# Three weight chunks per layer loaded once and split on chip, and a shorter warm-up, in a two-layer hybrid encoder

## What is computed

```python
def hybrid_layer(x, ...):                     # x: 512 tokens x 1024, float32
    z = rms_norm(x, g) @ w_in                 # 1024 -> 3712
    aq, ak, av, ag, bq, bk, bv, bg, ca, cb, cg = split(z)
    ya = neighbourhood_attention(aq, ak, av, rpb) * silu(ag)         # 4 heads
    yb = dilated_attention(rotary(bq), rotary(bk), bv) * silu(bg)    # 6 heads
    yc = conformer_conv(ca, cb, w_dw, ..., w_pw, b_pw) * silu(cg)    # 384 channels, 31 taps
    return x + concat([ya, yb, yc]) @ w_out   # 1024 -> 1024

def reference(x, ...):
    for l in range(2):
        x = hybrid_layer(x, ...)
    return rms_norm(x, final_g)
```

## Time and profile before

| | us |
|---|---|
| median of 3 runs | 513.06 (511.6 to 513.33) |
| profiled execution, its own time | 513.21 |
| its span | 511.4 |
| TensorE busy | 501.6 (98%) |
| VectorE busy | 365.1 (71%) |
| ScalarE busy | 275.5 (54%) |
| POOL busy | 164.0 (32%) |
| q0 (POOL's transfers) | 62.93 MB, 54.3% of the 16 DMA engines |
| q1 (SP's transfers) | 34.02 MB, 23.1% |

### The profile page before, as it was taken

One profiled execution on the slowest core, in us unless ns is written; L12 is line 12 of the kernel. 1 busy time (PEld: TensorE's weight loads), 2 busy tenths in 40 slices (PEclk: granted clock), 3 DMA queues, 4 the chain that ended last, 5 costly groups with the idle time before them and its releaser, 6 DMA issues.

```text
span 511.4 us, 10279 instructions
## 1 busy us (share of the span) xinstructions
PE 501.6 (98%) x3998; PEld 401.9 (79%) x3998; DVE 365.1 (71%) x741; ACT 275.5 (54%) x531; POOL 164.0 (32%) x224
## 2 busy tenths in 40 slices
PE   8999999999999999999999999999999999999995
PEld 6888877887777778788888887878787877778883
DVE  6999978899984666521539878887999656852424
ACT  6844667664664475524425447676646646752314
POOL 0013332221143557425411333222122355663101
PEclk9999999999999999999999999999999999999998
DMA  8715889669986997999502378975999979899964
GB/s 292 308 43 132 198 210 207 132 162 204 232 215 159 236 251 168 245 237 278 159 2 82 88 163 196 214 174 102 220 219 223 226 166 266 217 243 247 203 169 164
DMA packets 55120, 97.79 MB, mean 191 GB/s; under 512 B 19872, under 2 KB 33696, under 8 KB 55072
## 3 DMA queue, kind: packets, MB, share of 16 engines
q0 software_dynamic: 19648, 62.93, 54.3%
q1 hardware_dynamic: 35136, 34.02, 23.1%
q10 hardware_dynamic: 288, 0.19, 0.1%
HBM read 84.92 MB, written 5.90 MB: 178 GB/s over the span
## 4 chain that ended last, share of the span: by engine, by line
PE 93%; DMA 4%; issue 1%; ACT 0%; DVE 0%; POOL 0%; POOLq 0%; SPq 0%; ACTq 0%; DVEq 0%
PE acc L607 22%; PE acc L608 21%; PE acc L609 21%; PE sc L718 5%; PE tp L751 4%; DMA w_lo<-w_out 3%; PE misc L782 2%; PE sc L669 2%; PE sc L607 1%; PE sc L609 1%; PE sc L608 1%; PE sc L670 1%; PE sc L671 1%; PE misc L777 1%; PE acc L647 1%
## 5 line engine op out<-in xcount | busy, mean ns | idle before, releaser
L607 PE MATMUL acc<-act_hi,w_hi 128*128 128x512 f32 x480 | 194.5, 405 | 0.1
L608 PE MATMUL acc<-act_hi,w_lo 128*128 128x512 f32 x480 | 187.7, 391 | 0.0
L609 PE MATMUL acc<-act_lo,w_hi 128*128 128x512 f32 x480 | 187.1, 390 | 0.0
L607 PEld LDWEIGHTS acc<-act_hi,w_hi 128*128 128x128 f32 x480 | 90.2, 188 | 21.9 <-issue 3.9
L609 PEld LDWEIGHTS acc<-act_lo,w_hi 128*128 128x128 f32 x480 | 90.2, 188 | 19.9
L608 PEld LDWEIGHTS acc<-act_hi,w_lo 128*128 128x128 f32 x480 | 90.3, 188 | 17.1 <-issue 0.5
L877 ACT ACTIVATE w_lo<-w_hi 128x1024 fp32r<-128x1024 f32 (+1 forms) x62 | 61.9, 999 | 47.3 <-DMA w_hi<-w_out 38.0
L1320 DVE SCALAR_TENSOR_TENSOR y<-ub,par,y 128x512 f32<-128x512 f32 x90 | 70.0, 777 | 0.0
L1092 POOL DMA_DIRECT2D w_lo<-w_in x40 | 35.9, 897 | 106.2 <-ACT w_lo L877 105.5
L1320 DVE SCALAR_TENSOR_TENSOR ub<-ub,par 128x512 f32<-128x512 f32 x84 | 63.3, 754 | 0.0
L939 ACT ACTIVATE prob<-prob,nmx 128x384 f32<-128x384 f32 (+1 forms) x80 | 45.3, 567 | 25.1 <-DVE nmx L1342 24.9
(11 more groups left out here) (150 smaller groups left out, 718.7 us busy)
## 6 DMA issues: line engine op xcount, KB each, us to landing
w_hi<-w_in POOLq DMA_DIRECT2D x40, 512.0 KB, 5.8
w_lo<-w_in POOLq DMA_DIRECT2D x40, 512.0 KB, 6.1
w_hi<-w_out POOLq DMA_DIRECT2D x16, 512.0 KB, 6.4
w_lo<-w_out POOLq DMA_DIRECT2D x16, 512.0 KB, 7.0
pT<-w_in SPq DMA_DIRECT2D x15, 512.0 KB, 5.5
v<-v_way SPq DMA_DIRECT2D x40, 112.0 KB, 5.3
v_way<-vs SPq DMA_DIRECT2D x24, 112.0 KB, 5.6
gf<-nabias SPq DMA_DIRECT2D x20, 128.0 KB, 5.5
```

Source lines behind the costliest of these rows:

```text
L607: nc.tensor.matmul(to[:, :], w_hi[:, slot, k, :], a_hi[:, k, :], start=i == 0, stop=False)
L608: nc.tensor.matmul(to[:, :], w_lo[:, slot, k, :], a_hi[:, k, :], start=False, stop=False)
L609: last = nc.tensor.matmul(to[:, :], w_hi[:, slot, k, :], a_lo[:, k, :], start=False, stop=i == K - 1)
```

## The change

Chunks 27, 28 and 32 of each layer (`LATE`) leave POOL's queue. SP loads each once, unconverted, into the memory of v_far (`raw_late`): at its slots 27, 31 and 35 (`LATE_LOADS`), the first after the values of pair 2, each later one after the subtraction of the one before. ScalarE copies to w_hi at its slots 29, 33 and 38 (`late_split`), after the tile five chunks back is done; VectorE subtracts to w_lo at its slots 30, 34 and 39 (`late_rest`). POOL skips these chunks' two transfers and ScalarE their negation. The next layer's first v load waits for the last subtraction. POOL fills `ones` first instead of the identity, and TensorE runs nine warm-up products of ones with ones as soon as it is there, and waits for the other constants behind them.

```diff
--- before.py
+++ after.py
@@ -71,6 +71,16 @@
     return c < PRE
 
 
+LATE = (27, 28, 32)
+LATE_LOADS = {27: 27, 31: 28, 35: 32}
+LATE_HI = {29: 27, 33: 28, 38: 32}
+LATE_LO = {30: 27, 34: 28, 39: 32}
+
+
+def by_transfers(c):
+    return not by_engines(c) and c not in LATE
+
+
 PAIRS = 5
 DPAIRS = DIL_HEADS // 2
 UPP = 8
@@ -111,7 +121,7 @@
 PARTS_AT = {0: [0], 1: [1], 2: [2, 3], 5: [4, 5], KD: [6, 7]}
 X_GROUPS = [(0, 1), (1, 2), (2, 3), (3, 5), (5, 6), (6, 8)]
 X_ORDER = [list(range(KD))] + [[2, 3, 4, 0, 5, 6, 1, 7]] * (DEPTH - 1)
-WARM = 10
+WARM = 9
 
 EARLY = RAW_AHEAD
 SUMS = [(0, 1, 0), (2, 3, 0), (4, 5, 0), (0, 2, 2), (6, 7, 0), (4, 6, 5), (0, 4, 6)]
@@ -180,6 +190,7 @@
         prob = sb("prob", [P, PROBS, SEQ])
         pT = sb("pT", [P, 2, QT, SEQ])
 
+        raw_late = v_far[:, :, :, :].rearrange("p g i t -> p (g i t)").rearrange("p (k t) -> p k t", t=P)
         raw = pT[:, :, :, :].rearrange("p r a (b t) -> p (r a b) t", t=P).rearrange("p (r k) t -> p r k t", r=RAW)
         bias = sb("bias", [P, 2, NKEY])
         sq = sb("sq", [P, 2, SEQ])
@@ -226,6 +237,9 @@
         consts = sem("consts")
         tables = sem("tables")
         cleared = sem("cleared")
+        late_in = sem("late_in")
+        late_hi = sem("late_hi")
+        late_lo = sem("late_lo")
         hi_ready = sem("hi_ready")
         lo_ready = sem("lo_ready")
         part_in = [sem(f"part_in{i}") for i in range(len(PARTS))]
@@ -306,11 +320,15 @@
 
         def landed(l, c):
 
-            return 16 * sum(not by_engines(d % N_CH) for d in range(c % SPL, N_CH * l + c + 1, SPL))
+            return 16 * sum(by_transfers(d % N_CH) for d in range(c % SPL, N_CH * l + c + 1, SPL))
 
         def nth(l, c):
 
-            return sum(by_engines(d % N_CH) == by_engines(c) for d in range(N_CH * l + c + 1))
+            return sum(by_engines(d % N_CH) == by_engines(c) and d % N_CH not in LATE for d in range(N_CH * l + c + 1))
+
+        def nth_late(l, c):
+
+            return len(LATE) * l + LATE.index(c) + 1
 
         def nth_split(l, c):
 
@@ -486,6 +504,14 @@
                     sp.wait_ge(lo_ready, m - RAW + 1 - FIRST)
                 sp.dma_start(raw[:, m % RAW, :, :], w_in[l, c]).then_inc(raw_in[m % RAW], 16)
 
+            def load_late(l, c):
+
+                if c == LATE[0]:
+                    sp.wait_ge(pv_done, PAIRS * l + DPAIRS)
+                if nth_late(l, c) > 1:
+                    sp.wait_ge(late_lo, nth_late(l, c) - 1)
+                sp.dma_start(raw_late, chunk_src(l, c)[0]).then_inc(late_in, 16)
+
             def load_next(l, c):
                 f = follows(l, c + RAW_AHEAD)
                 if f is not None and by_engines(f[1]):
@@ -505,6 +531,8 @@
                 sp.wait_ge(v_stored, V_STORED * (PAIRS * l + g + 1))
                 if PAIRS * l + g >= 2:
                     sp.wait_ge(pv_done, PAIRS * l + max(g - 1, 0))
+                if l and g == 0:
+                    sp.wait_ge(late_lo, len(LATE) * l)
                 for j in range(QUADS):
                     to = v[BLK * j:BLK * (j + 1), g % 2]
                     if g < DPAIRS:
@@ -563,6 +591,8 @@
                         load_bias(l, n - BIAS_AT)
                     if DUNITS + 2 <= n < DUNITS + 2 + BIASES - BIAS_RING:
                         load_bias(l, n - DUNITS - 2 + BIAS_RING)
+                    if n in LATE_LOADS:
+                        load_late(l, LATE_LOADS[n])
                     if n in V_STORES:
                         store_v(l, V_STORES[n])
                     if n in V_LOADS:
@@ -618,6 +648,8 @@
                     pe.wait_ge(part_lo, part_with(c, 0))
                 elif by_engines(c):
                     pe.wait_ge(lo_ready, nth_split(l, c))
+                elif c in LATE:
+                    pe.wait_ge(late_lo, nth_late(l, c))
                 else:
                     pe.wait_ge(wlo_in[(N_CH * l + c) % SPL], landed(l, c))
                 if c in (2, 3):
@@ -664,7 +696,10 @@
                     c, w = OUT0 + KD // 2 * half + i // 2, slice(QT * (i % 2), QT * (i % 2 + 1))
                     slot = c % SPL
                     if a == 0 and i % 2 == 0:
-                        pe.wait_ge(wlo_in[slot], landed(LAST, c))
+                        if c in LATE:
+                            pe.wait_ge(late_lo, nth_late(LAST, c))
+                        else:
+                            pe.wait_ge(wlo_in[slot], landed(LAST, c))
                     to, rows, k = ROW_BANKS[half][a], slice(a * P, (a + 1) * P), K_ORDER[i]
                     nc.tensor.matmul(to[:, :], act_hi[:, k, rows], w_hi[:, slot, w, :], start=i == 0, stop=False)
                     nc.tensor.matmul(to[:, :], act_hi[:, k, rows], w_lo[:, slot, w, :], start=False, stop=False)
@@ -802,10 +837,11 @@
                 pe.wait_ge(add_done, ADD_L * l + LN_ADDS)
                 nc.tensor.matmul(misc[:, :], mean_w[:, :], ssq[:, :], start=True, stop=True).then_inc(misc_ready, 1)
 
+            pe.wait_ge(consts, 1)
+
+            for _ in range(WARM):
+                nc.tensor.matmul(misc[:, 0:P], ones[:, :], ones[:, :], start=True, stop=True)
             pe.wait_ge(consts, 5)
-
-            for _ in range(WARM):
-                nc.tensor.matmul(misc[:, 0:P], ones[:, :], ident[:, :], start=True, stop=True)
             for l in range(DEPTH):
                 if l == 0:
 
@@ -885,9 +921,14 @@
                 act.wait_ge(raw_in[m % RAW], 16 * (m // RAW + (m % RAW >= FIRST)))
                 nc.scalar.activation(w_hi[:, c % SPL, :, :], raw[:, m % RAW, :, :], ACT.Copy).then_inc(hi_ready, 1)
 
+            def late_split(l, c):
+                act.wait_ge(tile_done, N_CH * l + c - SPL + 1)
+                act.wait_ge(late_in, 16 * nth_late(l, c))
+                nc.scalar.activation(w_hi[:, c % SPL, :, :], raw_late, ACT.Copy).then_inc(late_hi, 1)
+
             def split_next(l, c):
                 f = follows(l, c + AHEAD)
-                if f is not None and (f[0] or f[1] >= EARLY):
+                if f is not None and f[1] not in LATE and (f[0] or f[1] >= EARLY):
                     (split_hi if by_engines(f[1]) else negate)(*f)
 
             def x_there(l, k):
@@ -1029,6 +1070,8 @@
                         exps(l, n)
                     if 0 < n <= UNITS:
                         norm(l, n - 1)
+                    if n in LATE_HI:
+                        late_split(l, LATE_HI[n])
                     if n < UNITS:
                         if n % 2 == 0:
                             split_next(l, tile_at(n)[0])
@@ -1093,12 +1136,12 @@
 
             def hi_next(l, c):
                 f = follows(l, c + CAST_AHEAD)
-                if f is not None and not by_engines(f[1]):
+                if f is not None and by_transfers(f[1]):
                     load_hi(*f)
 
             def lo_next(l, c):
                 f = follows(l, c + AHEAD)
-                if f is not None and not by_engines(f[1]):
+                if f is not None and by_transfers(f[1]):
                     load_lo(*f)
 
             def add_squares(l, k, base=0):
@@ -1126,8 +1169,8 @@
                     pool.dma_start(p_there(q)[BLK * j:BLK * (j + 1), NKEY * i:NKEY * (i + 1)],
                                    p_turned(q)[BLK * i:BLK * (i + 1), NKEY * j:NKEY * (j + 1)]).then_inc(p_moved_too[q], 16)
 
+            nc.gpsimd.memset(ones[:, :], 1.0).then_inc(consts, 1)
             nc.gpsimd.memset(ident[:, :], 0.0).then_inc(consts, 1)
-            nc.gpsimd.memset(ones[:, :], 1.0).then_inc(consts, 1)
             nc.gpsimd.memset(mean_w[:, :], 1.0 / CONV_CH).then_inc(consts, 1)
             nc.gpsimd.memset(nhalf[:, :], -0.5).then_inc(consts, 1)
             pool.wait_ge(consts, 4)
@@ -1416,6 +1459,11 @@
             def split_weights(l, c):
                 dve.wait_ge(hi_ready, nth_split(l, c))
                 weights_lo(l, c, 0, KD).then_inc(lo_ready, 1)
+
+            def late_rest(l, c):
+                dve.wait_ge(late_hi, nth_late(l, c))
+                nc.vector.tensor_tensor(w_lo[:, c % SPL, :, :], raw_late, w_hi[:, c % SPL, :, :], ALU.subtract)\
+                    .then_inc(late_lo, 1)
 
             def weights_next(l, c):
                 f = follows(l, c + AHEAD)
@@ -1537,6 +1585,8 @@
                             t = y[:, KD - CT + j, :]
                             nc.vector.tensor_scalar(t, t, parh[:, j:j + 1], parh[:, CT + j:CT + j + 1], ALU.mult,
                                                     ALU.add).then_inc(hn_ready, 1)
+                    if n in LATE_LO:
+                        late_rest(l, LATE_LO[n])
                     if n > UNITS:
                         pointwise(l, n - UNITS - 1)
                         y_lo(l, n - UNITS - 1)
```

## The result

| | before | after |
|---|---|---|
| median of six runs each, us | 513.07 (511.6 to 513.33) | 515.96 (514.88 to 516.75) |
| profiled execution / its span, us | 513.21 / 511.4 | 515.99 / 514.2 |

The ratio is 1.0064, 95% interval [1.0047, 1.0081]: 2.9 us slower, outside the range of 510.8 to 514.2. The gain at chunk 32 came as worked out. Most of the loss came at the program's end, where nothing of the diff stands, and a smaller part at the start.

A forecast was written before the change was run, and what follows sets the result against it. TensorE, busy 501.6 of 511.4 us, was taken to bound the kernel. Chunk 32's -1.15 us plus 0 each for split, SP queue and warm-up gave 512.06 from 513.21, 511.9 from the median; forecast 512.0, range 510.8 to 514.2.

The forecast's parts named there:

- chunk 32: First w_out chunk: TensorE's wait for its low half goes, gaining 1.05 us in layer 1 and 0.1 in layer 0.
- The tail: After TensorE's last product at 505 us: the diff doesn't touch it, so it stays as long as before.
- the split: ScalarE's copies and VectorE's six subtractions of 1.28 us: hidden in idle time, 0 taken, between 0 and 7.7 us.
- D: Waits at chunk 32: most executions have 1.5 us more in one layer, also removed, giving 510.5 us; chance 0.17.
- SP's queue: SP's late loads wait for subtractions ahead of the v store and P moves: 0 taken, ends 0 and 3 us.
- rival C: Chunk 28 lands late, SP's load 32 delays local P moves, TensorE's values wait: 515.5 us; chance 0.12.
- The warm-up: Program start: nine earlier products gain 0, since x, ScalarE and VectorE bind it; it can only lose through the clock.
- Rival B: At the start the clock rises later, so the first real products run slow: +0.85 us, 512.9 us; chance 0.18.

The follow-up runs named there:

- late_recip: late_only with VectorE's reciprocal in place of POOL's last four powers, the square root left out: 512.0 us, ratio 0.9982.
- late_series: The kernel before plus the three late chunks, old warm-up, last rows' powers finished by a VectorE polynomial instead of POOL: 512.4 us, ratio 0.9995.
- late_only: The kernel before with the three late chunks alone, keeping the old warm-up: 515.6 us, ratio 1.0055.
- fill28: late_only with 28 small transfers added at POOL's end: 519.52 us in one execution.
- noop12: late_only with twelve tiny memsets, no transfers, added on POOL after its last real transfer: 515.44 us, ratio 1.0045.
- fill20: late_only with twenty small transfers added at POOL's end: 515.3 us in one execution.

## Why the prediction was wrong

- **The tail, put at 0.** This step failed: "Everything else outside its busy time is the tail after its last product, at 505 us, which the diff doesn't touch", and "the tail as long as before". The tail grew by 3.15 us. The diff takes twelve transfers from POOL, and with them POOL's DRAIN went from 4012 to 7565 ns. Only 0.43 us lay between its end and SP's, a margin that the closing line of the trace showed and I hadn't read. late_recip and late_series take POOL's DRAIN off the end and with it the whole loss of the late chunks (3.6 and 3.2 us below late_only). In the step on the split, "POOL loses twelve issues and their waits; it follows TensorE's pace, so 0 or slightly below" stopped short of what those issues leave behind.
- **Chunk 32, -1.15 us:** right, in both parts. Layer 1 gave 1.00 (1.05), layer 0 0.10 (0.1), where act_lo is what is late next. But a wait of one execution is no constant, and there was some luck in the match: the five profiles without late chunks, before among them, have 0.5 to 2.1 us of waits for w_out's low halves. So D's premise had something to it; its 1.5 us more didn't show in a median.
- **The split, 0:** right. VectorE's subtraction starts at 178.47 and 187.68, and its idle time takes it. Timeline of VectorE, after, layer 0:

```profile
178.47 1.22 DVE L1465 TENSOR_TENSOR w_lo<-v_far,w_hi 128x1024 fp32r<-128x1024 f32 x1
...
187.68 1.22 DVE L1465 TENSOR_TENSOR w_lo<-v_far,w_hi 128x1024 fp32r<-128x1024 f32 x1
...
190.69 0.42 DVE L1385 CUSTOM_DVE_ANT_0 prob<-sc,bias 128x256 f32<-128x256 f32 x1 [0.81 <-PE sc L753]
```

  1.22 us each where I took 1.28, and of the 3.65 us of idle time in the earlier trace rows 0.81 is left.
- **SP's queue, 0:** right in this pair of traces, and closely. Timeline of SP, after:

```profile
179.72 0.33 SPq L513 DMA_DIRECT2D v_far<-w_in  x1
180.09 1.83 SPq L528 DMA_DIRECT2D v_way<-vs  x4
...
190.18 0.48 SPq L513 DMA_DIRECT2D v_far<-w_out  x1
```

  With the 0.73 us taken off by which everything is later here, the store begins at 179.4 (179.7 worked out) and load 32 at 189.5 (189.3). But the slack was as thin as worked out, and rival C came in other executions, where the prediction put it: late_only waits 0.6 us for the P moves of pair 4 in layer 0, and fill28 (its small transfers come only at 487 us) 1.4:

```profile
218.27 1.96 PE L830 MATMUL misc<-pT,v 128*32 128x128 f32 x64 [1.42 <-DMA pT<-zc]
```

  Ahead of pair 3's values of layer 0, where the five profiles without late chunks all have a gap of 0.32 us, fill28, noop12, fill20 and late_recip have 1.11, 0.84, 0.78 and 0.49; the profile names no releaser there. So the queue costs 0 in most executions and up to about 2 us in one.
- **The warm-up, 0:** mis-sized. The start lost 1.18 us to before's in this pair, and more against every other profile with the old warm-up. Rival B's figure was 0.85, for a late rise; what came was an early rise and a fall. By the Trainium skill, TensorE: Matmul & The Clock Gate, Part 1, idling gives the clock back; the trace agrees (idle from 4.80 to 6.32, half speed from 7.66). That B's time of 512.9 is what the change would have taken without the longer end (515.99 - 3.15 = 512.84) is luck in part: it holds the 0.45 us that this execution of before lost at 133 us.

With the measured terms the sum closes: 513.21 - 1.10 + 1.18 - 0.45 + 3.15 = 515.99.

## What to carry to other kernels

Before a change to which engine issues transfers, read the closing instructions of every engine, with their ends: the program ends with the last of them. Here POOL, which issues transfers and also had the last small operation, closed with a DRAIN of 4 us that ended 0.43 us before the last engine, and any growth beyond that went into the time. Giving the last rows' small operations to another engine let the DRAIN begin 20 us early, and its length then cost nothing. Count on the time of such a replacement: it cost up to 1.5 us in some executions. And compare a single profile with others of its kind before putting a difference down to a change: a stall of 0.45 us and waits of 0 to 2 us came and went between executions. An earlier warm-up gained nothing measurable here; with an idle gap of 1.5 us or more behind it, both profiles started more than a microsecond late.

## What the runs showed of the hardware

- POOL's closing DRAIN, begun behind the last rows, is the same to 2 ns in every profile of the same sequence of transfers (7565, 7565, 7567; 4012, 4014, 4014). Twelve small transfers at the end put 982 ns on it with and without late chunks, and eight more 655 (fill20 to fill28): 82 ns each. But from twelve to twenty it falls by 2289, and it can get longer with fewer transfers (4012 with 180, 9363 with 176).
- Begun within 3 us of POOL's last issue it ends 5.0 to 5.1 us after that transfer's last packet (168 transfers, three profiles) or 2.1 (180, one).
- The two profiles with nine warm-up products and 1.5 to 1.8 us of idling behind them lost the clock for 3.4 us; the two with fourteen and no idling did not, nor did two that idled 0.5 and 0.7 us.
